# A two-block transformer on one core: latents of the attention layer from unscaled H by token blocks, turned before their norms, and another order of the small work ahead of the heads

## The reference, cut to what matters

```python
def _rmsnorm_2(x, gain):
    y = xf * lax.rsqrt(jnp.mean(xf * xf, axis=-1, keepdims=True) + RMS_EPS)
    return (y * gain.astype(jnp.float32)).astype(x.dtype)

def _mla_mixer(h, ...):                                  # h = _rmsnorm_2(x, norm_mix[1]), 256 x 1024
    c_q, c_kv, k_rope = jnp.split(h @ w_in, [256, 512], axis=-1)
    q = (_rmsnorm_2(c_q, q_a_norm) @ w_q_up).reshape(B, S, 8, 192)
    kv = (_rmsnorm_2(c_kv, kv_a_norm) @ w_kv_up).reshape(B, S, 8, 128 + 128)
    k_nope, v = jnp.split(kv, [MLA_NOPE], axis=-1)
    ...
    q = _rope_tail(_rmsnorm_2(q, q_norm), cos, sin)
    k = _rope_tail(_rmsnorm_2(k, k_norm), cos, sin)
    o = _causal_block_attention(q, k, v)                 # softmax attention, 8 heads
    return o.reshape(B, S, 1024) @ w_out
...
    x = x + y                                            # each layer and each FFN adds to x
```

## Time and profile before

| | us |
|---|---|
| runs | 1576.96, 1583.41, 1587.16 |
| median | 1583.41 |
| the profiled execution | 1583.74 |
| its span, first to last instruction | 1582.4 |
| mean granted TensorE clock | 0.952 of full speed |

### The profile page before, as it was taken

The page is one execution under the profiler, slowest core; times in us unless marked ns, Lnnn a source line. Parts: engine busy times, 40 slices in busy tenths (PEclk is TensorE's granted clock), DMA queues, the critical chain, the costliest instruction groups (busy, mean ns, idle before and its releaser), DMA issues.

```text
span 1582.4 us, 27526 instructions
## 1 busy us (share of the span) xinstructions
PE 1430.1 (90%) x11669; PEld 1206.2 (76%) x11669; DVE 861.9 (54%) x1529; ACT 686.4 (43%) x1188; POOL 10.6 (1%) x10
## 2 busy tenths in 40 slices
PE   7999999999899767777877789999999998999998
PEld 6999899899865334434433589989999885899997
DVE  5785453565522111111111569857888766678876
ACT  6443554543432111111111676455555564555553
POOL 1000000000000000000000100000000000000000
PEclk9999999999989998899897999989999997999999
DMA  7454354477999999999999454234555532245552
GB/s 234 158 163 157 110 163 131 163 269 273 347 407 420 419 419 418 420 419 420 419 421 420 158 160 134 80 107 160 187 195 197 163 105 80 80 161 195 194 176 101
DMA packets 173713, 372.05 MB, mean 235 GB/s; under 512 B 6912, under 2 KB 141184, under 8 KB 149008
## 3 DMA queue, kind: packets, MB, share of 16 engines
q1 hardware_dynamic: 173584, 370.21, 63.4%
HBM read 369.14 MB, written 1.05 MB: 234 GB/s over the span
## 4 chain that ended last, share of the span: by engine, by line
PE 66%; DMA 22%; DVE 5%; ACT 4%; issue 1%; SPq 1%; DVEq 0%; ACTq 0%
PE bank L583 17%; PE bank L584 16%; PE bank L585 16%; DMA wu<-in_expert_w_down_dram 16%; DMA wu<-in_expert_w_up_dram 3%; PE bank L1702 3%; PE bank L814 3%; PE bank L1674 2%; DVE lo L547 2%; PE bank L1740 2%; ACT hi L536 1%; DMA raw<-in_w_in_dram 1%; PE bank L948 1%; PE bank L1755 1%; PE bank L923 1%
## 5 line engine op out<-in xcount | busy, mean ns | idle before, releaser
L547 DVE TENSOR_TENSOR lo<-raw,hi 128x1024 fp32r<-128x1024 f32 (+2 forms) x315 | 375.7, 1216 | 202.4 <-ACT hi L536 201.7
L583 PE MATMUL bank<-XH,hi 128*128 128x256 f32 x1416 | 404.8, 286 | 4.6 <-DVE lo L547 2.2
L584 PE MATMUL bank<-XL,hi 128*128 128x256 f32 x1416 | 400.0, 282 | 0.0
L585 PE MATMUL bank<-XH,lo 128*128 128x256 f32 x1416 | 399.9, 282 | 0.0
L536 ACT ACTIVATE hi<-raw 128x1024 fp32r<-128x1024 f32 (+2 forms) x315 | 321.0, 1049 | 120.5 <-PE bank L585 41.4
L583 PEld LDWEIGHTS bank<-XH,hi 128*128 128x128 f32 x1416 | 270.7, 191 | 12.3 <-issue 7.1
L584 PEld LDWEIGHTS bank<-XL,hi 128*128 128x128 f32 x1416 | 270.6, 191 | 0.8
L585 PEld LDWEIGHTS bank<-XH,lo 128*128 128x128 f32 x1416 | 270.6, 191 | 0.0
L1702 PE MATMUL bank<-wu,xg 128*32 128x256 f32 x2048 | 171.0, 437 | 49.3 <-DMA wu<-in_expert_w_up_dram 45.9
L1702 PEld LDWEIGHTS bank<-wu,xg 128*32 128x32 f32 x2048 | 72.1, 122 | 123.3 <-DMA wu<-in_expert_w_up_dram 63.3
L1740 PE MATMUL bank<-wu,hidT 128*32 128x256 f32 x1024 | 72.8, 408 | 40.1 <-DMA wu<-in_expert_w_down_dram 34.9
(11 more groups left out here) (355 smaller groups left out, 2234.6 us busy)
## 6 DMA issues: line engine op xcount, KB each, us to landing
wu<-in_expert_w_gate_dram SPq DMA_DIRECT2D x64, 1024.0 KB, 27.0
wu<-in_expert_w_up_dram SPq DMA_DIRECT2D x64, 1024.0 KB, 26.7
wu<-in_expert_w_down_dram SPq DMA_DIRECT2D x64, 1024.0 KB, 27.0
raw<-in_w_in_dram SPq DMA_DIRECT2D x44, 1024.0 KB, 5.1
raw<-in_ffn_w_up_dram SPq DMA_DIRECT2D x44, 1024.0 KB, 5.0
raw<-in_ffn_w_down_dram SPq DMA_DIRECT2D x22, 1024.0 KB, 5.0
raw<-in_hgrn_w_in_dram SPq DMA_DIRECT2D x16, 1024.0 KB, 5.4
raw<-in_w_branch_ret_dram SPq DMA_DIRECT2D x8, 1024.0 KB, 6.5
```

Source lines behind the costliest of these rows:

```text
L547: dve.tensor_tensor(lo_of(u), v, hi_of(u), ALU.subtract).then_inc(*WL.inc(u))
L583: pe.matmul(dst, first[0], first[1], start=start, stop=False)
L584: pe.matmul(dst, second[0], second[1], start=False, stop=False)
L585: return pe.matmul(dst, third[0], third[1], start=False, stop=stop)
```

## The change

The attention layer's latents are made from H without its norm factor. Each half of a token block of H is turned as soon as it is added (`pe_block`, four transposes; ACT and DVE write its XH and XL, 128 x 128 each). The latents are made for one token block at a time, and turned as they are copied out, without a norm. The two factors, H's and the latent's, become one (`cs2[12:16]`; since the rows were not scaled, the latent's epsilon is multiplied by the mean square of H), and ACT multiplies it in where k, v and q are copied out. The shared rotary part has H's factor alone. Weight units are split where needed, no longer four ahead; the units of O0 and O1 are split in steps 4 to 7 of the heads. The root of q's second half, its squares and its rotation move into steps 1 and 2 of the heads. The adds of the last FFN keep their place.

```diff
@@ pe_ffn, the last product of the FFN
+                        if l == 0 and (t, c) == (1, 0):
+                            pe_block(0, 0)
@@ new; the four additions to H are moved out of dve_ffn to dve_ffn_result(l, t, c)
+        BLOCK_BANK = {(0, 0): 3, (0, 1): 4, (1, 0): 5, (1, 1): 6}
+        def pe_block(t, c):
+            ...
+            pe.wait_ge(*FF[0].dve.got("H", t, c))
+            for j in range(4):
+                k = 4 * c + j
+                done = pe.transpose(b.ap[:, j * P:(j + 1) * P], H[:, t, k * P:(k + 1) * P], ident)
+            done.then_inc(*NORM.pe.inc(5, "t", t, c))
+        def act_block(t, c):
+            act.wait_ge(*NORM.pe.got(5, "t", t, c))
+            for j in range(4):
+                k = 4 * c + j
+                act.activation(XH[:, k, t * P:(t + 1) * P], b_[BLOCK_BANK[t, c]][:, j * P:(j + 1) * P], ACT.Copy,
+                               scale=PR("norm_mix_2", 8 + k)).then_inc(*NORM.act.inc(5, "h", t, k))
+        def dve_block(t, c):
+            for j in range(4):
+                k = 4 * c + j
+                dve.wait_ge(*NORM.act.got(5, "h", t, 4 * c + 3))
+                dve.scalar_tensor_tensor(XL[:, k, t * P:(t + 1) * P], ...).then_inc(*NORM.dve.inc(5, "l", t, k))
@@ pe_mla
-            pe_norm(5, xs5)
-            for j in (1, 2, 0):
-                pe_wide(unit2(C_TILE[j]), C_BANK[j], 8, C_WIDTH[j], XH, XL, x, [(X.act, ("c", j))], [turn_kv()] if j == 0 else [])
+            pe_block(0, 1)
+            latent(1, 0)
+            pe_block(1, 0)
+            pe_block(1, 1)
+            latent(2, 0)
+            latent(1, 1)
+            latent(0, 0)
+            latent(0, 1)
+            turn_latent(1)
+            latent(2, 1)
+            turn_latent(0)
             up("k", 0, 1, 512)
-            turn_latent(0)
             up("k", 1, 1, 512)
@@ act_mla, copies out of k, v and q
-                act_split(unit2(K_TILE[i]) + 2 + AHEAD)
-                        act.activation(Kt[:, t, h0:h0 + 2, 0:P], b4[:, :, 0:P], ACT.Copy)...
+                        act.wait_ge(*X.dve.got("crstd"))
+                        act.activation(Kt[:, t, h0:h0 + 2, 0:P], b4[:, :, 0:P], ACT.Copy, scale=cs2[:, 14 + t:15 + t])...
@@ act_mla, order
+            act_block(0, 0)
+            act_block(0, 1)
+            act_split(unit2(C_TILE[0]) + 2)
+            act_block(1, 0)
+            act_block(1, 1)
+            for t in range(2):
+                act.activation(xs5[:, t, :], H[:, t, :], ACT.Square, accum_out=st[:, 40 + t:41 + t])...
+            act.activation(st[:, 50:52], st[:, 40:42], ACT.Sqrt, bias=epst[:, 0:1], scale=1.0 / D)...
             latent(1)
+            act_split(unit2(K_TILE[0]) + 2)
+            latent(0)
+            turn_latent(1)
+            act.activation(cs2[:, 8:12], cs2[:, 8:12], ACT.Sqrt).then_inc(*X.act.inc("croot"))
+            rope_latent()
+            turn_latent(0)
+            act_split(unit2(K_TILE[1]) + 2)
             k_up(0)
-            turn_latent(0)
+            act_split(unit2(Q_TILE[0]) + 2)
             k_scale(0)
             k_up(1)
+            act_split(unit2(Q_TILE[1]) + 2)
             k_scale(1)
             q_up(0)
-            q_scale(0)
             for h in range(4):
                 turn_k(h)
             q_up(1)
-            q_scale(1)
+            q_scale(0)
             for h in range(4, 8):
                 turn_k(h)
             for h in range(12):
...
+                if h == 1:
+                    q_scale(1)
                 if 1 <= h < 9:
                     score(h - 1)
                 if h >= 4:
                     attend(h - 4)
+                    if h < 8:
+                        act_split(unit2(O_TILE) + h - 3)
@@ dve_mla, order
+            for t, c in ((0, 0), (0, 1), (1, 0)):
+                dve_ffn_result(0, t, c)
+            dve_block(0, 0)
+            dve_block(0, 1)
+            dve_ffn_result(0, 1, 1)
+            dve_split(unit2(C_TILE[0]) + 2)
+            dve_block(1, 0)
+            dve_block(1, 1)
...
             for h in range(12):
                 if h < 8:
                     turn_q(h)
+                if h == 1:
+                    q_up(1)
                 if 1 <= h < 9:
                     score(h - 1)
+                if h == 2:
+                    dve.wait_ge(*X.dve.got("rope", "q", 0, 1))
+                    q_scale(1)
                 if h >= 4:
                     attend(h - 4)
+                    if h < 8:
+                        dve_split(unit2(O_TILE) + h - 3)
```

More of the change, by code:

```diff
@@ L2440, in pe_mla, with latent @@
         def pe_mla():
-            X, x = ML, normed(5)
-            pe_norm(5, xs5)
+            X = ML
+            def latent(j, t):
+                u, n, b = unit2(C_TILE[j]), C_WIDTH[j], bank[C_BANK[j]]
+                for s, key in b.taken if t == 0 else []:
+                    pe.wait_ge(*s.got(*key))
+                for k in range(8):
+                    pe.wait_ge(*WH.got(u + k // 4))
+                    pe.wait_ge(*WL.got(u + k // 4))
+                    pe.wait_ge(*NORM.act.got(5, "h", t, k))
+                    pe.wait_ge(*NORM.dve.got(5, "l", t, k))
+                    done = three(b.ap[:, t * n:(t + 1) * n], hi_of(u + k // 4)[:, k % 4, :], lo_of(u + k // 4)[:, k % 4, :],
+                                 XH[:, k, t * P:(t + 1) * P], XL[:, k, t * P:(t + 1) * P], True, k == 0, k == 7)
+                    if t == 1 and k % 4 == 3:
+                        done.then_inc(*WU.inc(u + k // 4))
+                b.taken = [(X.act, ("c", j))]
             def turn_latent(j):
@@ L2619, in q_up @@
                         act.activation(Qt[:, t, h0:h0 + 2, :], b_[up_bank("q", i, c, t)][:, 0:384].rearrange("p (h d) -> p h d", h=2),
-                                       ACT.Copy).then_inc(*X.act.inc("q", i, c, t))
+                                       ACT.Copy, scale=cs2[:, 12 + t:13 + t]).then_inc(*X.act.inc("q", i, c, t))
             def q_scale(i):
@@ L2653, in attend @@
                 act.activation(OH3[:, h, :], b_[6 + h % 2][:, 0:T], ACT.Copy).then_inc(*X.act.inc("OH", h))
-            latent(1)
[L2656 to L2659, removed]
+            act_block(0, 0)
[3 more added lines that the diff above has]
+            act_block(1, 1)
+            for t in range(2):
+                act.activation(xs5[:, t, :], H[:, t, :], ACT.Square, accum_out=st[:, 40 + t:41 + t]).then_inc(*X.act.inc("sqH", t))
+            act.wait_ge(*X.act.got("sqH", 1))
+            act.activation(st[:, 50:52], st[:, 40:42], ACT.Sqrt, bias=epst[:, 0:1], scale=1.0 / D).then_inc(*X.act.inc("root"))
+            latent(1)
+            act_split(unit2(K_TILE[0]) + 2)
+            latent(0)
+            turn_latent(1)
+            act.wait_ge(*X.dve.got("cmean", 0))
+            act.activation(cs2[:, 8:12], cs2[:, 8:12], ACT.Sqrt).then_inc(*X.act.inc("croot"))
+            rope_latent()
+            turn_latent(0)
+            act_split(unit2(K_TILE[1]) + 2)
             k_up(0)
-            turn_latent(0)
+            act_split(unit2(Q_TILE[0]) + 2)
             k_scale(0)
             k_up(1)
+            act_split(unit2(Q_TILE[1]) + 2)
             k_scale(1)
             q_up(0)
-            q_scale(0)
             for h in range(4):
@@ L2692, in sum_sq, with latent @@
                                          accum_out=acc).then_inc(*X.dve.inc("sq", n))
[L2694 to L2695 removed]
+            def latent(j):
                 dve.wait_ge(*X.act.got("c", j))
@@ L2863, in after @@
             dve_ffn(0, [dve_angles2()])
-            dve_mla([(FF[0].dve, ("H", 1, 1))])
+            dve_mla()
             dve_ffn(1, [])
+            for t in range(2):
+                for c in range(2):
+                    dve_ffn_result(1, t, c)
         return before, fallback, after
```

95 lines of the change are left out of this document (43 added, 52 removed).

## The result

The changed kernel takes 1572.98 us at the median of seven runs (1569.95 to 1579.08), the kernel before 1580.16 (seven runs), 7.2 us more. The ratio over all of these runs is 0.9949, with a 95% interval of 0.9925 to 0.9973, or 8.1 us. A second comparison (six runs against eleven, medians 1571.03 and 1582.11) gave 0.9925 (0.9912 to 0.9938), 11.9 us. The forecast was 1574.0, or 9.7 us less than the profiled execution before.

What follows compares the result with a forecast made beforehand. The chain lay on PE for 66% and DMA for 22%; the edited stretch had two holes and a slow-clock part. Terms 1 to 4 gain 14.7 us, less 5 for the clock: 9.7 off 1583.74, so 1574.0, range 1570 to 1579.

Steps and rivals of the forecast that it cites:

- Term 1, the first hole: From the FFN's end to the latents: first latent matmul at 1267.35 instead of 1272.7, with a 0.35 us PE wait.
- Term 2, the latents: Latents through q's end at full clock: k's first matmul 5.95 us earlier, q's end 6.4 earlier, weights split in time.
- Rival 3: Weights come late in k or q: ACT and DVE 3 us later than forecast make PE stand 1.8 us; 1576; chance 0.10.
- Term 3, the second hole: From q's end to the first score: 4.2 us of ACT's list remain of 11.4; first score 13.5 us earlier.
- Term 4, the heads: Heads at full clock: DVE paces, steps with a unit take 4.75 us; eighth mask 14.7 us earlier.
- Term 5, the clock: In the heads: clock falls in the third step, two and a half slow steps, plus 5 us.
- 1 (the clock stays): Through the heads the clock stays at 1.00, so the sum is terms 1 to 4: 1569.0; chance 0.17.
- 2 (it falls at once): Transposes and waits behind q's end drop the clock, first three scores slow: gain 8 us or less, 1576.5; chance 0.12.
- 4 (low through the heads): Clock falls before the first score and stays at 1.2 GHz until the heads end: 1584.7, slower; chance 0.06.

Runs made afterwards that it cites:

- filler_turns: The changed kernel with PE's wait for the rotation, behind the third score, filled with 24 transposes that nothing reads; ratio to the kernel before 0.9932.
- units_end: The changed kernel with q's second-half squares and rotation moved to DVE's waits, and all four O0 and O1 units in steps 8 to 11; ratio to the kernel before 0.9886.
- units_ahead: The changed kernel with the four units of O0 and O1 split where they were before, at the copies of q; ratio to the kernel before 0.9932.
- rot_units: rot_early with the two units of O1 moved from steps 6 and 7 into steps 8 and 9 of the heads; ratio to the kernel before 0.9883.
- front_only: The changed kernel with the old order ahead of the heads (units, both roots and rotation there); ratios to the kernel before 0.9972 and 0.9968.
- changed_again: The changed kernel as it is, measured and profiled a second time; ratio to the kernel before 0.9925.
- rot_early: The changed kernel with q's second-half squares moved ahead of the first head's copy and its rotation behind the second head's copy; ratio to the kernel before 0.9913.

## Why the prediction was right, point by point

**The sum.** 9.7 us was forecast. The medians differ by 7.2 us, the two ratios give 8.1 us (4.3 to 11.9) and 11.9 us (9.8 to 13.9), and the two traces, from the mark to the span's end, 10.0 and 12.3. That the median lies only 1 us from 1574.0 is in part luck: the forecast started from a median of 1583.41 for the kernel before, and the seven runs beside the changed kernel have 1580.16.

**Term 1, the first hole.** First latent matmul 6.60 us behind the mark, 6.61 forecast. PE's wait for the second group's XL was 0.17 us, where 0.35 was forecast.

**Term 2, the latents.** The gain at k was 5.83 us, against 5.95; at q's end 6.27, against 6.4. Two pieces of 64 columns did not disturb the clock. One entry of the sum is too low by its own figures: a first piece of 2.9 us with a wait of 0.35 is 3.25, not 2.95, and it took 3.35. The groups of transposes gave most of it back, 0.35 to 0.41 us each where 0.45 was taken. The weights were in time: k's second tile had its two `lo` at 1295.8 and 1297.0, and PE, without a wait, took the first up at 1297.30 and the second 0.7 us behind it: 1.5 and 1.0 us to spare, where the prediction had 1.2 at the tighter one. Rival 3 did not occur.

**Term 3, the second hole.** First score 13.48 us earlier, 13.5 forecast. What was left is ACT's list, busy for 4.17 of 4.34 us.

**Term 4, the heads.** Where the clock stays up to the eighth score (filler_turns), the eighth mask stands at 84.24 us, against 84.56. Two errors cancel in that: the first step, with the load of the exponent's table, took 3.74 us instead of 3.3, and the last one with a unit 4.33 instead of 4.75. That a unit costs a step 1.45 us (4.75 less 3.3) is confirmed by units_end: 1.27 to 1.44 less in each of the four steps. Its half-sentence that they are a loss there is right as well, but only against a better place: ahead of the heads they cost the clock (units_ahead); behind the last mask all four together cost the stretch 1.3 us (units_end against filler_turns) instead of 5.5 in the steps.

**Term 5, the clock.** The fall came in the third step, in the wait for the rotation that the prediction named or 1.8 us behind it, and in the first profile the rise 4 us behind the first attend. Against filler_turns it cost 3.7 us in the stretch and 1.1 behind it in the first profile, 2.6 and nothing in the second; 5 was taken. That 5 does not come out of the prediction's prices: two and a half steps make 3.6 us if the fourth score's 1.0 is the first of them, and 5.4 if it comes besides. The distribution was wrong too: in the heads of the first profile 2.5 us (1.76 in one step, 0.70 in the next), not 5. Two steps were slow, not two and a half, and in the second the clock was back 1.5 us ahead of its mask. The rest comes from a second fall, in PE's wait of 2.55 us behind the eighth mask, which the prediction did not have. That the two errors nearly cancel is luck. The low clock of 8 to 15 us within the heads that was named as the sign came in the first profile (10 us), not in the second (7).

**The rivals.** 1 (the clock stays) is wrong for this kernel, and right as a mechanism once the wait is gone: rot_units. 2 (it falls at once) is wrong; the clock held 1.00 through turns and waits up to 1327, and filler_turns speaks against its ground. 4 (low through the heads) did not occur. Its beginning, a fall before the first score, did in units_ahead, whose hole is 6.77 us. But the clock rose there within the heads, as the prediction had it.

## What to carry to other kernels

Where a row of small steps is paced by one engine, work moved into them out of a hole costs its full length; move it to where that engine waits for another one, here ahead of the first mask and behind the last. A short wait of TensorE can cost more than itself when the clock falls in it or just behind it and stays low through the next steps, so look for it in the clock of the windows, and take it away by reordering before anything else. When a single run's time scatters by more than the effect, compare traces from a mark ahead of the change to one behind it, and profile a kernel twice where the clock is low.

## What the runs showed of the hardware

- The length of a low-clock stretch differs between executions of one kernel whose instructions stand at the same places: 17 and 27 us (front_only), 10 and 7 us (changed). It was worth up to 4.6 us.
- Transposes filling a wait of 2.6 us held 2.4 GHz (granted clock 1.00) just as four matmuls did, in one profile each.
- A fall does not need to stand in a wait: in changed_again it came 1.8 us behind one of 2.60 us through which the clock was 1.00. Nor does it need a long single one: in rot_early it came behind three waits of 0.40, 0.89 and 1.40 us in steps of 4.7 us. In rot_units, with waits of 0.40, 0.89 and 1.63 us, none came; these runs do not show what decides it.
